# Reading the delta-rule sample states: the state as moving operand on four column tiles of TensorE, then a transpose

## What is computed

```python
def gated_delta_recurrence(q, k, v, g, beta, s0):
    '''S_t = exp(g_t)(I - beta_t k_t k_t^T) S_{t-1} + beta_t k_t v_t^T, o_t = S_t^T q_t'''
...
y_sample, hg_s, gdn_s, conv_s, pool_s = trunk(x_sample, state_hgrn, state_gdn, state_gdn_conv, state_pool, PAST_LEN, prm)
```

## Time and profile before

| | |
|---|---|
| median of three runs | 1101.53 us (1099.68 to 1103.32) |
| the profiled execution | 1102.12 us |
| its span in the trace | 1100.4 us |
| TensorE busy | 1066.8 us (97%) |
| VectorE, ScalarE, GpSimd busy | 676.0, 521.1, 79.1 us |
| mean granted clock of TensorE | 0.988 of full |

### The profile page before, as it was taken

One profiled execution on the slowest core, in us unless ns is written; L12 is line 12 of the kernel. 1 busy time (PEld: TensorE's weight loads), 2 busy tenths in 40 slices (PEclk: granted clock), 3 DMA queues, 4 the chain that ended last, 5 costly groups with the idle time before them and its releaser, 6 DMA issues.

```text
span 1100.4 us, 21542 instructions
## 1 busy us (share of the span) xinstructions
PE 1066.8 (97%) x8463; PEld 1042.2 (95%) x8463; DVE 676.0 (61%) x872; ACT 521.1 (47%) x703; POOL 79.1 (7%) x157
## 2 busy tenths in 40 slices
PE   6999999989899998999999999999999999999998
PEld 5999999979799996999999999999999989999997
DVE  5666654577555655776666448666644886666543
ACT  5544443466555453454444337444433644444334
POOL 8100000110000200110000002000000120000001
PEclk9999999999889999899999999999999999999999
DMA  6666655887477421466665557666555436665551
GB/s 196 194 184 178 181 180 174 150 198 148 110 102 145 136 76 48 128 188 173 178 183 172 191 173 210 192 175 185 175 180 181 135 114 197 177 184 175 182 179 40
DMA packets 135062, 177.92 MB, mean 162 GB/s; under 512 B 5806, under 2 KB 120574, under 8 KB 134992
## 3 DMA queue, kind: packets, MB, share of 16 engines
q1 hardware_dynamic: 131616, 165.78, 53.7%
q0 software_dynamic: 3328, 11.38, 3.6%
q10 hardware_dynamic: 64, 0.02, 0.0%
HBM read 171.19 MB, written 6.52 MB: 161 GB/s over the span
## 4 chain that ended last, share of the span: by engine, by line
PE 85%; DVE 8%; ACT 3%; issue 2%; DMA 2%; ACTq 0%; SPq 0%; DVEq 0%
PE ps L1506 25%; PE ps L1507 25%; PE ps L1508 24%; ACT w_hi L517 2%; DVE xw_lo L1043 1%; PE ps L1334 1%; DVE w_lo L1018 1%; DMA raw<-in_w_in_even 1%; PE ps L1341 1%; DVE x L1032 1%; PE ps L1323 1%; DVE rstd L1049 1%; DVE PT L979 1%; PE ps L1304 1%; PE ps L1353 1%
## 5 line engine op out<-in xcount | busy, mean ns | idle before, releaser
L1018 DVE TENSOR_TENSOR w_lo<-raw,w_hi 128x1024 fp32r<-128x1024 f32 x312 | 380.9, 1224 | 302.6 <-ACT w_hi L517 300.8
L517 ACT CAST w_hi<-raw 128x1024 fp32r<-128x1024 f32 x312 | 325.7, 1049 | 450.5 <-PE ps L1508 431.0
L1506 PE MATMUL ps<-xw_hi,w_hi 128*128 128x264 f32 x1504 | 429.9, 286 | 3.5 <-ACT rstd L539 1.3
L1507 PE MATMUL ps<-xw_lo,w_hi 128*128 128x264 f32 x1504 | 428.9, 285 | 0.0
L1508 PE MATMUL ps<-xw_hi,w_lo 128*128 128x264 f32 x1504 | 428.1, 285 | 0.0
L1506 PEld LDWEIGHTS ps<-xw_hi,w_hi 128*128 128x128 f32 x1504 | 284.0, 189 | 6.5 <-issue 3.9
L1508 PEld LDWEIGHTS ps<-xw_hi,w_lo 128*128 128x128 f32 x1504 | 283.2, 188 | 0.0
L1507 PEld LDWEIGHTS ps<-xw_lo,w_hi 128*128 128x128 f32 x1504 | 283.0, 188 | 0.1
L1508 PE MATMUL ps<-a_hi,w_lo 128*128 (+1 forms) x704 | 200.3, 285 | 0.0
L1506 PE MATMUL ps<-a_hi,w_hi 128*128 (+1 forms) x704 | 200.0, 284 | 0.0
L1507 PE MATMUL ps<-a_lo,w_hi 128*128 (+1 forms) x704 | 200.0, 284 | 0.0
(11 more groups left out here) (337 smaller groups left out, 830.4 us busy)
## 6 DMA issues: line engine op xcount, KB each, us to landing
raw<-in_ffn_w_gate SPq DMA_DIRECT2D x88, 512.0 KB, 3.8
raw<-in_ffn_w_up SPq DMA_DIRECT2D x88, 512.0 KB, 3.8
raw<-in_ffn_w_down SPq DMA_DIRECT2D x88, 512.0 KB, 3.4
raw<-in_w_in_even SPq DMA_DIRECT2D x32, 512.0 KB, 7.3
raw<-in_w_out_even SPq DMA_DIRECT2D x8, 512.0 KB, 4.6
raw<-in_pool_w_in SPq DMA_DIRECT2D x8, 512.0 KB, 3.5
out<-SBUFS POOLq DMA_DIRECT2D x4, 512.0 KB, 3.8
PT<-in_x_prompt SPq DMA_DIRECT2D x2, 512.0 KB
```

What stands on the lines that cost most here:

```text
L517: nc.scalar.copy(w_hi[:, w % SPL, :], raw[:, w % RAW, :]).then_inc(hi_done, 1)
L1018: nc.vector.tensor_tensor(w_lo[:, w % SPL, :], raw[:, w % RAW, :], w_hi[:, w % SPL, :].bitcast(F32), ALU.subtract).then_inc(lo_done, 1)
L1506: mm(out, wh, hi, start=first, stop=False)
L1507: mm(out, wh, lo, start=False, stop=False)
```

## The change

The reads of the 32 delta-rule states swap their operands. The stationary operand is now 128 by 4 columns out of a small tile `QK4` and the moving operand is the state, 128 columns. `QK4` holds for each head, for each half of the samples (bh) and each sample in it (bl) four columns: query and key in columns 2bh and 2bh+1, and zeros in the other two. The result of sample bl of both halves lands in partitions 32bl to 32bl+3 of PSUM bank 6, in the head's 128 columns, and the two halves are summed there (the zeros keep them apart). So four samples sit on four column tiles of 32 of the array, and there are again 32 matmuls, now in one piece behind slot 28 and no longer in four pieces of eight. The result lies with the value along the free axis, so ScalarE copies the bank (128 by 512) to `READS`, and TensorE transposes it back with four transposes behind slot 29.

GpSimd clears `QK4` once; VectorE fills it with four small copies, and takes the query part of the reads into SBUF (`rdq`) before it forms the new values. `QK4` and `READS` lie in `KT`, which is written only later. Besides that, pairs of semaphores are merged into one that counts to two (`kk_mm` and `kq_mm` into `gram_mm`, `cum_mm` and `brow` into `cum_mm`, `hs1_mm` and `hs2_mm`, `s1_mm` and `ks_mm`, `vn0` and `vn1`, `vn0_mm` and `vn1_mm`), each waited for at the same place as before; an increment that nobody waited for (`fold_ok`) goes. The diff without these:

```diff
--- before.py
+++ after.py
@@ -137,6 +137,9 @@
+        KTf = KT.rearrange("p i n -> p (i n)")
+        QK4 = KTf[:, 128:256].rearrange("p (h bh bl m) -> p h bh bl m", h=4, bh=2, bl=4)
+        READS = KTf[:, 256:768]
@@ -410,7 +413,10 @@
-            slots(28, 31)
+            slots(28, 30)
+            act.wait_ge(st("samp_read"), 1)
+            A.copy(READS, ps[:, 6, :]).then_inc(st("read_rows"), 1)
+            slots(30, 31)
@@ -744,7 +750,18 @@
-            rd = ps[:, 7, 32:96].rearrange("p (h b y) -> p h b y", h=4, y=2)
+            dve.wait_ge(st("qk_zero"), 1)
+            for bh in range(2):
+                for y in range(2):
+                    ins = V.tensor_copy(QK4[:, :, bh, :, 2 * bh + y],
+                                        C[:, 4 * y:4 * y + 4, PROMPT + 4 * bh:PROMPT + 4 * bh + 4])
+            ins.then_inc(st("qk4"), 1)
+            rd = ps[:, 6, :].rearrange("p (h bl m) -> p h bl m", h=4, bl=4)[:, :, :, 0:4]\
+                .rearrange("p h bl (bh y) -> p h bh bl y", bh=2)
+            rdq = SMALL[:, 352:384]
+
+            def hbb(ap):
+                return ap.rearrange("p h (bh bl) -> p h bh bl", bh=2)
@@ -794,8 +811,9 @@
-            dve.wait_ge(st("samp_read"), 4)
-            link(V.tensor_tensor(hb(tmp2), C[:, 8:12, smp], rd[:, :, :, 1], ALU.subtract))
+            dve.wait_ge(st("read_T"), 1)
+            V.tensor_copy(hbb(hb(rdq)), rd[:, :, :, :, 0])
+            link(V.tensor_tensor(hbb(hb(tmp2)), hbb(C[:, 8:12, smp]), rd[:, :, :, :, 1], ALU.subtract))
@@ -889,7 +907,7 @@
-            dve.wait_ge(st("samp_read"), 8)
+            dve.wait_ge(st("samp_read"), 5)
-            V.tensor_tensor(O[:, 4:8, smp], rd[:, :, :, 0], hb(WV[:, 2, :]), ALU.add).then_inc(st("so"), 1)
+            V.tensor_tensor(O[:, 4:8, smp], hb(rdq), hb(WV[:, 2, :]), ALU.add).then_inc(st("so"), 1)
@@ -1296,14 +1313,21 @@
-            for h in range(4):
-                if h:
-                    slots(27 + h, 28 + h)
-                pe.wait_ge(st("samp_dec"), h + 1)
-                for b in range(NSAMP):
-                    ins = mm(ps[:, 7, 32 + 16 * h + 2 * b:34 + 16 * h + 2 * b], SV(h)[:, b, :],
-                             C[:, h:h + 5:4, PROMPT + b], start=True, stop=True)
-                ins.then_inc(st("samp_read"), 1)
+            slots(28, 29)
+            pe.wait_ge(st("samp_dec"), 4)
+            pe.wait_ge(st("qk4"), 1)
+            for h in range(4):
+                for bh in range(2):
+                    for bl in range(4):
+                        ins = mm(ps[32 * bl:32 * bl + 4, 6, h * P:(h + 1) * P], QK4[:, h, bh, bl, :],
+                                 SV(h)[:, 4 * bh + bl, :], start=bh == 0, stop=bh == 1)
+            ins.then_inc(st("samp_read"), 1)
+            slots(29, 30)
+            pe.wait_ge(st("read_rows"), 1)
+            for h in range(4):
+                ins = tr(ps[:, 6, h * P:(h + 1) * P], READS[:, h * P:(h + 1) * P], ident[:, :])
+            ins.then_inc(st("read_T"), 1)
+            slots(30, 31)
@@ -1755,6 +1779,7 @@
             load_state(2)
             load_state(3)
+            G.memset(KTf[:, 128:256], 0.0).then_inc(st("qk_zero"), 1)
             pool.wait_ge(st("crow"), 1)
```

More of the change, by code:

```diff
@@ L368, in even_scalar @@
             A.copy(SMALL[:, 128:160], ps[:, 7, 32:64]).then_inc(st("bs"), 1)
-            act.wait_ge(st("brow"), 1)
+            act.wait_ge(st("cum_mm"), 2)
             A.activation(QE[:, :, :], psA[:, 4:8, :], ACT.Exp)
@@ L452, in even_scalar @@
             A.copy(HKT, psC).then_inc(st("hkt"), 1)
-            act.wait_ge(st("hs1_mm"), 1)
+            act.wait_ge(st("hs_mm"), 1)
             A.copy(HS1, ps[:, 2, :]).then_inc(st("hs1"), 1)
@@ L726, in even_vector @@
             slots(22, 24)
-            dve.wait_ge(st("kk_mm"), 1)
+            dve.wait_ge(st("gram_mm"), 1)
             for i in range(8):
@@ L733, in even_vector @@
             slots(24, 25)
-            dve.wait_ge(st("kq_mm"), 1)
+            dve.wait_ge(st("gram_mm"), 2)
             V.tensor_tensor(DEC[:, :, :], DEC[:, :, :], psB, ALU.mult).then_inc(st("aqk"), 1)
@@ L881, in even_vector @@
                 .then_inc(st("kt"), 1)
-            dve.wait_ge(st("vn0_mm"), 1)
+            dve.wait_ge(st("vn_mm"), 1)
             V.tensor_tensor(VN[:, 0:4, :], psB[:, 0:4, :], beta[:, 0:4].unsqueeze(2).broadcast_to([P, 4, P]), ALU.mult)\
-                .then_inc(st("vn0"), 1)
+                .then_inc(st("vn"), 1)
             samples_stored(dve, (2, 3))
             dve.wait_ge(st("samp_kq_mm"), 2)
-            dve.wait_ge(st("samp_read"), 8)
+            dve.wait_ge(st("samp_read"), 5)
             V.tensor_tensor(WV[:, 2, :], ps[:, 7, 128:160], vn, ALU.mult)
             link(V.tensor_tensor(hb(WV[:, 4, :]), hb(ps[:, 7, 160:192]), PT[:, 8:12, smp], ALU.mult))
-            V.tensor_tensor(O[:, 4:8, smp], rd[:, :, :, 0], hb(WV[:, 2, :]), ALU.add).then_inc(st("so"), 1)
+            V.tensor_tensor(O[:, 4:8, smp], hb(rdq), hb(WV[:, 2, :]), ALU.add).then_inc(st("so"), 1)
             V.tensor_tensor(O[:, 0:4, smp], hb(ps[:, 7, 0:32]), hb(WV[:, 4, :]), ALU.add).then_inc(st("so"), 1)
@@ L899, in even_vector @@
             link(V.tensor_tensor(hs2v, hs1v, totc, ALU.mult))
-            dve.wait_ge(st("hs2_mm"), 1)
+            dve.wait_ge(st("hs_mm"), 2)
             V.tensor_tensor(HS2, HS2, ps[:, 3, :], ALU.add).then_inc(st("hs2"), 1)
-            dve.wait_ge(st("ks_mm"), 1)
+            dve.wait_ge(st("s1_mm"), 2)
             dve.wait_ge(st("ebt"), 1)
@@ L906, in even_vector @@
             V.tensor_tensor(VT[:, 4:8, :], VT[:, 4:8, :], VN[:, 4:8, :], ALU.subtract).then_inc(st("rhs1"), 1)
-            dve.wait_ge(st("vn1_mm"), 1)
+            dve.wait_ge(st("vn_mm"), 2)
             dve.wait_ge(st("rhs1"), 1)
             V.tensor_tensor(VN[:, 4:8, :], psB[:, 0:4, :], beta[:, 4:8].unsqueeze(2).broadcast_to([P, 4, P]), ALU.mult)\
-                .then_inc(st("vn1"), 1)
+                .then_inc(st("vn"), 1)
             link(V.tensor_tensor(S2[:, :, :], S1[:, :, :], SMALL[:, 68:72].unsqueeze(2).broadcast_to([P, 4, P]),
@@ L1147, in _ @@
                     link(ins)
-            ins.then_inc(st("fold_ok"), 1)
             for gi, w in enumerate(WINDOWS):
@@ L1237, in even_tensor @@
                 ins = mm(psA[:, i, :], gt[:, c, 0, h:h + 1].broadcast_to([P, P]), upper[:, :], start=True, stop=True)
-            ins.then_inc(st("brow"), 1)
+            ins.then_inc(st("cum_mm"), 1)
             pe.wait_ge(st("norm_sq"), 1)
@@ L1263, in even_tensor @@
                 ins = mm(psA[:, i, :], kk, kk, start=True, stop=True)
-            ins.then_inc(st("kk_mm"), 1)
+            ins.then_inc(st("gram_mm"), 1)
             for i, (c, h) in enumerate(ch):
@@ L1267, in even_tensor @@
                          stop=True)
-            ins.then_inc(st("kq_mm"), 1)
+            ins.then_inc(st("gram_mm"), 1)
             slots(22, 26)
@@ L1381, in even_tensor @@
                 ins = mm(psB[:, h, :], U[:, h, :], VT[:, h, :], start=True, stop=True)
-            ins.then_inc(st("vn0_mm"), 1)
+            ins.then_inc(st("vn_mm"), 1)
             pe.wait_ge(st("hvt"), 1)
@@ L1389, in even_tensor @@
                              stop=True)
-                ins.then_inc(st(("hs1_mm", "hs2_mm")[y]), 1)
+                ins.then_inc(st("hs_mm"), 1)
             pe.wait_ge(st("kt"), 1)
-            pe.wait_ge(st("vn0"), 1)
+            pe.wait_ge(st("vn"), 1)
             for h in range(4):
@@ L1405, in even_tensor @@
                 ins = mm(psA[:, 4 + h, :], C[:, 4 + h, P:2 * P], S1[:, h, :], start=True, stop=True)
-            ins.then_inc(st("ks_mm"), 1)
+            ins.then_inc(st("s1_mm"), 1)
             pe.wait_ge(st("rhs1"), 1)
@@ L1409, in even_tensor @@
                 ins = mm(psB[:, h, :], U[:, 4 + h, :], VT[:, 4 + h, :], start=True, stop=True)
-            ins.then_inc(st("vn1_mm"), 1)
+            ins.then_inc(st("vn_mm"), 1)
             def mean_squares(y, bank):
@@ L1426, in even_tensor @@
             mean_squares(0, 0)
-            pe.wait_ge(st("vn1"), 1)
+            pe.wait_ge(st("vn"), 2)
             pe.wait_ge(st("qe"), 1)
```

## The result

The changed kernel takes 1095.81 us (median of five, 1094.09 to 1096.29) against 1101.53 before (by now also a median of five, 1099.68 to 1103.32), ratio 0.995 with a 95% interval of 0.9935 to 0.9965.

The account below looks back on a forecast made before the run. TensorE, busy throughout the reads' stretch, was taken as the bound; -6.80 (old reads) + 3.58 (new reads) + 0.44 (transposes) = -2.8 us, from 1101.53 to 1098.7 us, range 1096.6 to 1102.6.

Parts of the forecast that it names:

- What goes: The 32 old reads, in four pieces on TensorE's path, disappear: 6.80 us saved.
- The new reads: 32 matmuls on four column tiles between slots 28 and 29, two at a time: 3.58 us added.
- The failed step: In the new reads, two records per matmul in program order let only two tiles work at once: 0.112 us per matmul.
- The upper bound: New reads gain nothing from their tiles: 7.16 us for 32, sum +0.8, 1102.3 us; chance 0.15.
- the lower one: New reads with all four tiles working at once take a quarter: 1.79 us.
- Transposes back: Four fp32 transposes of 128 by 128 on TensorE's path, returning the reads' results: 0.44 us added.
- Interruptions: First record after fp32 work takes 0.23 us, not 0.13; four breaks before and after, column-tile switching free: no change.
- The copies, the wait for GpSimd, `rdq` and the earlier demand for slots: Side work around slots 28 to 31 stays hidden; ScalarE's copy to READS ends with 2.3 us to spare.
- Bound by the rate of small records: Rival: the reads' 64 records go no faster than 0.071 us each, 4.5 us; sum -1.8, 1099.7 us; chance 0.15.
- The clock falls after the reads: Rival: TensorE drops to half speed after the reads, costing 1.7 us; sum -1.1, 1100.4 us; chance 0.05.
- some 0.3 us of scatter of a median on either side: Whole-kernel median: allowance of 0.3 us each side, widening 1096.9 and 1102.3 us into the range.
- the rival with 0.20, four tiles at once: All four tiles work together in the new reads: 1.79 us, sum -4.6, 1096.9 us; chance 0.20.

Follow-up runs that it names:

- e3_tile_order: Changed kernel with the two halves of the samples innermost, so a tile's four records stand behind one another; reads 1.88 us, kernel 1093.03 us (one run).
- e6_tile_by_tile: Changed kernel with the reads ordered tile by tile, all 16 records of one tile before the next; reads 5.79 us, kernel 1099.49 us (one run).
- e9_two_heads_a_tile: Changed kernel with 8 records on each tile in turn, then the same again; reads 4.07 us, kernel 1099.19 us (one run).

## Why the prediction was wrong

The place was right: TensorE was the bound around the reads, and its saved time went through to the end. The terms:

- *What goes*, 6.80 us: right, the old reads stand in the profile of the kernel with only the merged semaphores with the same 1.76 and 1.68.
- *The new reads*, 3.58 us: wrong, 1.86 measured. The failed step is "If matmuls start in program order, as they do everywhere in the chain, ... tile 2 cannot run beside tile 0. Two at a time, then". The chain of before has no work on several column tiles, so its order said nothing of them. `e3_tile_order` (1.88 us) and the starts in `e6_tile_by_tile` show that a record for a free tile does not wait for an earlier one of a busy tile; `e6_tile_by_tile` and `e9_two_heads_a_tile` show the limit that there is, four records to a tile (5.79 and 4.07 us), which the changed kernel's order never meets. The upper bound, 7.16 us without overlap, was close (7.08), and so was the lower one, 1.79. The rule of the Trainium skill that I weighed (TensorE: Matmul & The Clock Gate, Part 3) was right in that tiles overlap (3.8 times on four here) and, as far as starts go, not in its order: the runs decide here.
- *Transposes back*, 0.44: right, 0.44. *Interruptions*: the first record behind the reads takes 0.32 us, where 0.23 was reckoned, so the way back from column tiles costs about a tenth of a microsecond and not nothing. In sum "Nothing changes" holds all the same (12.02 us for the four slots against 12.07): the first record behind the four transposes takes 0.13 us in the chain, where 0.23 was reckoned.
- The copies, the wait for GpSimd, `rdq` and the earlier demand for slots: all hidden, as forecast. That the copy had 2.3 us to spare, the very figure of the forecast, is luck: with reads of 1.79 us the prediction's own times left 2.0 (346.2 to 348.2), and the load came earlier than reckoned (the cast began at 343.68, not at 344.5).
- *Bound by the rate of small records* is excluded: 64 records in 1.86 us are 0.029 us each. *The clock falls after the reads* did not happen: the stretch with them and the ten microseconds behind it, from 340 to 360 us, were at 1.00.

With 1.86 in its place the sum is -4.5 us. From the first median that is 1097.0, inside my range; the measured 1095.81 lay below it because the second thing was wrong too: "some 0.3 us of scatter of a median on either side". Single runs of the kernel before reach over 6.6 us, its median of five was 1101.53 and those of 23, 17 and 11 runs 1100.50, 1100.18 and 1100.95. From 1100.5 the sum gives 1096.0, near both medians of the changed kernel. The case that came true was the rival with 0.20, four tiles at once; what was held against it, two records per matmul in program order, is the failed step.

The extra 1.1 us of the first comparison are, as far as the record goes, scatter. By its time, the median of the five runs before (1101.53) lies among the runs at the lowest clock, 0.988, and the median of the five changed ones had 0.991; the clocks of those five runs before are not on record. Of the 1.3 us by which the two traces differ outside the stretch from the key-query product to the last `evac`, 0.65 stand already in the first load's landing, in code that did not change:

```profile
1.75 4.65 DMA PT<-in_x_sample
```

```profile
1.75 4.00 DMA PT<-in_x_sample
```

## What to carry to other kernels

Where a 128 by 128 operand meets one or two vectors in fp32, let the big one move and the vectors stand, on four column tiles: 32 such reads went from 6.8 to 1.9 us, at the price of a copy and four short transposes. Order them so that no tile gets more than four records (two fp32 matmuls) in a row. And before a gain of half a per cent is weighed, look where the granted clock differs between executions: here the scatter was as large as the change, and with full rows in the broadcasts most of it was gone, and 4 us with it.

## What was not expected of the hardware

- Records for different column tiles start out of program order: with four records of each tile in a row the 64 still take 1.88 us, 0.029 us a record, while one tile alone needs 0.111.
- A tile takes four records and then holds up what comes behind: 5.79 us tile by tile, 4.07 with eight each.
- TensorE's granted clock fell to half (0.50, 1.2 of 2.4 GHz) with TensorE busy all the time, behind broadcasts of 8 rows, in nine of ten profiled executions; with all rows it stayed at 1.00 in both.
